# Root, tables, residual and last scaling around three RMS norms of a two-block float32 kernel: the epilogues reordered, and TensorE given products of ones

## What is computed

```python
def rmsnorm(x, g):
    return x * rsqrt(mean(x * x, axis=-1) + 1e-6) * g
# block 1, layer 0: convolution branch and gated linear recurrence, merged by w_out (tiles "ya", "yb")
x = x + gate0 * out_0
h1 = rmsnorm(x, norm_g[1]) * (1 + scale1) + shift1       # here called the first norm
# block 1, layer 1: pooling over a grid (tiles "ou", "og", "grp", "oa", "ob")
x = rmsnorm(x + gate1 * out_1, final_g)
# block 2: token mixers on h2 and a context (tiles "f" ... "gb2", "pa", "pb", "wo")
x = x + gate2 * mix
h3 = rmsnorm(x, g_ffn) * (1 + sc3) + sh3                 # here called the second norm
x = x + gate3 * ((silu(h3 @ w_a) * (h3 @ w_b)) @ w_down) # tiles "ua", "ub", then "d0", "d1", "d2"
out = rmsnorm(x, g_final)                                # the end
```

## Time and profile before

| what | value |
|---|---|
| median of 3 runs (lowest, highest) | 950.0 us (949.25, 951.11) |
| the profiled execution: its time, its span | 950.38 us, 948.6 us |
| PE busy; weight loads (PEld) | 891.7 us (94%); 833.6 us (88%) |
| DVE busy | 706.0 us (74%) |
| ACT busy; POOL busy | 500.6 us (53%); 142.0 us (15%) |
| mean granted clock of PE | 0.976 |
| the chain that ended last, by engine | PE 65%, DVE 20%, ACT 5%, issue 4%, DMA 3%, POOL 2% |

### The profile page before, as it was taken

One profiled execution on the slowest core, in us unless ns is written; L12 is line 12 of the kernel. 1 busy time (PEld: TensorE's weight loads), 2 busy tenths in 40 slices (PEclk: granted clock), 3 DMA queues, 4 the chain that ended last, 5 costly groups with the idle time before them and its releaser, 6 DMA issues.

```text
span 948.6 us, 17209 instructions
## 1 busy us (share of the span) xinstructions
PE 891.7 (94%) x7048; PEld 833.6 (88%) x7048; DVE 706.0 (74%) x1016; ACT 500.6 (53%) x717; POOL 142.0 (15%) x254
## 2 busy tenths in 40 slices
PE   6999999989997999899998999989999799999995
PEld 4788777778996998789998999979999699999995
DVE  4787678899876799988558985686985886666453
ACT  5475888796445544235543474563534454444441
POOL 0004675600011001400301100300001100000000
PEclk9999999999998999999999999989999799999998
DMA  9835987975575668775528844635556366666661
GB/s 370 354 133 161 291 271 230 296 281 177 160 264 200 222 224 278 255 266 178 178 73 286 290 131 137 201 94 194 157 179 178 121 235 179 186 188 181 198 200 47
DMA packets 56013, 195.53 MB, mean 206 GB/s; under 512 B 7936, under 2 KB 9088, under 8 KB 54528
## 3 DMA queue, kind: packets, MB, share of 16 engines
q1 hardware_dynamic: 40320, 147.83, 48.5%
q0 software_dynamic: 15616, 46.61, 14.5%
HBM read 188.70 MB, written 1.05 MB: 200 GB/s over the span
## 4 chain that ended last, share of the span: by engine, by line
PE 65%; DVE 20%; ACT 5%; issue 4%; DMA 3%; POOL 2%; DVEq 0%; ACTq 0%; SPq 0%; POOLq 0%
PE ps L570 18%; PE ps L571 18%; PE ps L572 18%; DVE w_lo L1333 6%; PE ps L721 3%; ACT w_hi L941 2%; DVE modw L1367 2%; POOL shifts L458 2%; DMA modw<-in_mod_w 2%; PE px L641 1%; DVE dump L1699 1%; DMA raw<-in_stream 1%; PE ps L652 1%; PE px L527 1%; DVE li L1347 1%
## 5 line engine op out<-in xcount | busy, mean ns | idle before, releaser
L1333 DVE TENSOR_TENSOR w_lo<-raw,w_hi 128x1024 fp32r<-128x1024 f32 x232 | 281.5, 1227 | 134.0 <-ACT w_hi L941 133.5
L941 ACT ACTIVATE w_hi<-raw 128x1024 fp32r<-128x1024 f32 x232 | 243.6, 1055 | 125.3 <-DMA raw<-in_stream 125.1
L570 PE MATMUL ps<-h_hi,w_hi 128*128 128x256 f32 (+1 forms) x928 | 278.8, 300 | 25.4 <-DVE w_lo L1333 12.1
L571 PE MATMUL ps<-h_lo,w_hi 128*128 128x256 f32 (+1 forms) x928 | 273.4, 295 | 0.0
L572 PE MATMUL ps<-h_hi,w_lo 128*128 128x256 f32 (+1 forms) x928 | 273.2, 294 | 0.0
L570 PEld LDWEIGHTS ps<-h_hi,w_hi 128*128 128x128 f32 x928 | 181.7, 196 | 37.8 <-DVE w_lo L1333 16.8
L571 PEld LDWEIGHTS ps<-h_lo,w_hi 128*128 128x128 f32 x928 | 181.9, 196 | 3.6 <-issue 1.2
L572 PEld LDWEIGHTS ps<-h_hi,w_lo 128*128 128x128 f32 x928 | 181.8, 196 | 2.6
L570 PE MATMUL ps<-h2o_hi,w_hi 128*128 128x256 f32 x352 | 103.5, 294 | 8.5 <-DVE w_lo L1333 8.5
L571 PE MATMUL ps<-h2o_lo,w_hi 128*128 128x256 f32 x352 | 101.4, 288 | 0.0
L572 PE MATMUL ps<-h2o_hi,w_lo 128*128 128x256 f32 x352 | 101.3, 288 | 0.0
(11 more groups left out here) (328 smaller groups left out, 1732.5 us busy)
## 6 DMA issues: line engine op xcount, KB each, us to landing
raw<-in_stream SPq DMA_DIRECT2D x252, 512.0 KB, 3.8
modw<-in_mod_w POOLq DMA_DIRECT2D x80, 512.0 KB, 6.2
m<-in_mod_w SPq DMA_DIRECT2D x8, 1024.0 KB, 18.1
shifts<-upad POOLq DMA_DIRECT2D x128, 35.5 KB, 4.3
c_row<-in_c_rows SPq DMA_DIRECT2D x3, 512.0 KB, 9.2
ctxT<-in_ctxT SPq DMA_DIRECT2D x1, 1024.0 KB, 4.9
x<-in_xT SPq DMA_DIRECT2D x1, 1024.0 KB, 7.0
ctx2T<-in_ctx2T SPq DMA_DIRECT2D x1, 1024.0 KB, 5.7
```

The costliest lines, as they stand in the source:

```text
L570: pe.matmul(o, wh, hi, start=start, stop=False)
L571: pe.matmul(o, wh, lo, start=False, stop=False)
L941: act.activation(w_hi[split[0] % HI_RING][:], raw[n % RING][:], ACT.Copy).then_inc(w_hi_ready, 1)
L1333: v.tensor_tensor(w_lo[n % RING][:], raw[n % RING][:], w_hi[split[0] % HI_RING][:].bitcast(F32), ALU.subtract).then_inc(w_lo_ready, 1)
```

## The change

1. **Root from the bank.** For the norms behind "yb", "og" (a norm of the second context), "wo" and "d2" DVE's mean plus epsilon is gone. ACT takes the root straight from PSUM, with 1/D as scale and a new column of 1e-6 as bias.
2. **Table ahead.** The dummy root that loads ACT's table is issued before the eight squares (for "og": directly before the root, without a wait between them) and no longer after them.
3. **Last residual ahead of the low half.** In `add_to_x` for the last slab of "yb" and "wo" DVE adds first, and makes the low half of the fourth tile of the next layer after it. For "ob" nothing changes, and for "d2" there is no low half left by then.
4. **Wide end.** ACT makes xg = x * g_final_2 in 8 instructions, one behind each square of "d2". DVE then multiplies xg by the reciprocal in three instructions, of 2, 3 and 3 slabs, and SP writes three times, 256, 384 and 384 KB.
5. **Ones.** At the first and the second norm PE multiplies the matrix of ones by itself (128 columns, into the bank px[1], which nobody reads) 4 times before `two_chunks` and 14 times after it.

The counts of the semaphore var_ready are lowered in the other norms to match.

```diff
+        xg = at("xg", W + 8, [KT, T])
...
-            for k in range(KT):
-                sp.wait_ge(stored, k + 1)
-                sp.dma_start(out[:, k, :], x[:, k, :]).then_inc(out_done, 16)
-            sp.wait_ge(out_done, 16 * KT)
+            for n, (first, end) in enumerate(((0, 2), (2, 5), (5, 8))):
+                sp.wait_ge(stored, n + 1)
+                sp.dma_start(out[:, first:end, :], xg[:, first:end, :]).then_inc(out_done, 16)
+            sp.wait_ge(out_done, 16 * 3)
...
+            def keep_busy(n):
+
+                for _ in range(n):
+                    pe.matmul(px[1][:, 0:P], ones, ones, start=True, stop=True)
...
+            keep_busy(4)
             two_chunks(px[0], sq1, 1, 3 * KT)
+            keep_busy(14)
             h1 = (lambda k: h1_hi[:, k, :], lambda k: h1_lo[:, k, :])
             side_by_side([("ou", t) for t in range(4)], *h1, (h_ready, 0))
...
+            keep_busy(4)
             two_chunks(px[0], sq4, 7, 7 * KT)
+            keep_busy(14)
...
+            def root_table():
+
+                S.do(act.activation(warm, warm, ACT.Sqrt))
+
+            def root_of_mean(stat, t, bank):
+
+                act.wait_ge(stat_done, stat)
+                act.activation(t, bank[:, 0:T], ACT.Sqrt, scale=1.0 / D, bias=eps_col).then_inc(sd_ready, 1)
...
+            root_table()
             for t in range(KT):
                 done("yb", t)
                 squares("yb", t, sq1)
-            highs("ou", 3)
-
-            sqrt_of(4, vr1[:])
+
+            root_of_mean(5, vr1[:], px[0])
             shifted(0, h1_hi, t1, shift1)
...
+            root_table()
             for t in range(KT):
                 done("wo", t)
                 squares("wo", t, sq4)
-            sqrt_of(10, v4[:, 0, :])
+            root_of_mean(9, v4[:, 0, :], px[0])
             shifted(3 * KT, h3_hi, t4, sh3)
...
+            root_table()
             for t in range(KT):
                 done("d2", t)
                 squares("d0", t, sq5)
-            sqrt_of(11, v4[:, 0, :])
+                act.activation(xg[:, t, :], x[:, t, :], ACT.Identity, scale=col("g_final_2", t)).then_inc(xg_ready, 1)
+            root_of_mean(10, v4[:, 0, :], px[0])
...
             def add_to_x(name, t, gate):
 
-                done(name, t)
+                if t < KT - 1 or name == "ob":
+                    ahead(name, t)
+                v.wait_ge(tile_done, TILE[(name, t)] + 1)
...
-            def rstd(stat, bank, width, eps, t, dst, var_n):
-
-                v.wait_ge(stat_done, stat)
-                v.tensor_scalar(t, bank, 1.0 / width, eps, ALU.mult, ALU.add).then_inc(var_ready, 1)
-                v.wait_ge(sd_ready, var_n)
+            def rstd(n, t, dst):
+
+                v.wait_ge(sd_ready, n)
                 S.do(v.reciprocal(dst, t))
                 S.sync()
...
-            rstd(10, px[0][:, 0:T], D, EPS, v4[:, 0, :], v4[:, 1, :], 11)
-            for k in range(KT):
-                v.scalar_tensor_tensor(out=x[:, k, :], in0=x[:, k, :], scalar=col("g_final_2", k), in1=v4[:, 1, :],
-                                       op0=ALU.mult, op1=ALU.mult).then_inc(stored, 1)
+            rstd(11, v4[:, 0, :], v4[:, 1, :])
+            v.wait_ge(xg_ready, KT)
+            for first, end in ((0, 2), (2, 5), (5, 8)):
+                by_token = v4[:, 1, :].rearrange("p (n t) -> p n t", n=1).to_broadcast([P, end - first, T])
+                v.tensor_tensor(xg[:, first:end, :], xg[:, first:end, :], by_token, ALU.mult).then_inc(stored, 1)
```

More of the change, by code:

```diff
@@ L361, in build @@
         out_done = sem("out_done")
+        xg_ready = sem("xg_ready")
         modA = columns(2 * KT).rearrange("p (k w) -> p k w", w=2)
@@ L372, in build @@
         ccs = columns(2 * KT)
-        warm = columns(1)
+        warm, eps_col = columns(1), columns(1)
         sc1, gate1 = columns(KT), columns(KT)
@@ L855, in _ @@
             thirds("ga2", 0, *own2)
-            pe.wait_ge(var_ready, 8)
+            pe.wait_ge(var_ready, 6)
             pe.wait_ge(hg_dve, 10)
@@ L885, in _ @@
             pe.wait_ge(in_sgu, 48)
-            pe.wait_ge(var_ready, 9)
+            pe.wait_ge(var_ready, 7)
             for g in range(HEADS):
@@ L1183, in _ @@
                 act.activation(og[:, t, :], psum_of("og", t)[:, 0:T], ACT.Silu).then_inc(free_of("og", t), 1)
-            sqrt_of(5, vr[:, 0, :])
+            root_table()
+            root_of_mean(6, vr[:, 0, :], px[1])
             for t in range(KT):
@@ L1195, in _ @@
             highs("f", 3)
-            sqrt_of(6, vr[:, 1, :])
-            act.wait_ge(var_ready, 7)
+            sqrt_of(4, vr[:, 1, :])
+            act.wait_ge(var_ready, 5)
             act.activation(vr[:, 2, :], vr[:, 2, :], ACT.Sqrt).then_inc(sd_ready, 1)
@@ L1275, in _ @@
             exps(1)
-            sqrt_of(8, lnv[:, 3, :])
+            sqrt_of(6, lnv[:, 3, :])
             out_of("o", 2, og2, ACT.Silu)
@@ L1300, in _ @@
             highs("gb2", 3)
-            sqrt_of(9, ors[:])
+            sqrt_of(7, ors[:])
             for t in range(KT):
@@ L1372, in _ @@
             v.memset(ones, 1.0).then_inc(cc_clear, 1)
+            v.memset(eps_col, EPS6)
             v.memset(warm, 1.0).then_inc(cc_clear, 1)
@@ L1669, in _ @@
             v.memset(opad[:, :, :, 8 + GRID_W:PW], 0.0).then_inc(pads_ready, 1)
-            rstd(5, px[0][:, 0:T], D, EPS6, vr1[:], vr1[:], 4)
+            rstd(4, vr1[:], vr1[:])
             modulate(0, x, vr1[:], sc1, shift1, t1, h1_hi, h1_lo)
@@ L1725, in _ @@
                     second_mods(g, s, 0, mod, t, True)
-            rstd(6, px[1][:, 0:T], D, EPS, vr[:, 0, :], vr[:, 3, :], 5)
+            rstd(5, vr[:, 0, :], vr[:, 3, :])
             for t in range(KT + 1):
@@ L1771, in _ @@
             v.tensor_scalar(vr[:, 0, :], vr[:, 1, :], EPS, None, ALU.mult).then_inc(var_ready, 1)
-            v.wait_ge(var_ready, 6)
+            v.wait_ge(var_ready, 4)
             v.wait_ge(stat_done, 8)
@@ L2033, in _ @@
             lows("ub", 1)
-            rstd(9, px[0][:, 0:T], D, EPS, v4[:, 0, :], v4[:, 1, :], 10)
+            rstd(10, v4[:, 0, :], v4[:, 1, :])
             modulate(3 * KT, x, v4[:, 1, :], sc3, sh3, t4, h3_hi, h3_lo)
```

## The result

The change takes 943.95 us (median of 4 runs, 942.41 to 944.51), the kernel before 949.62 beside it (4 runs). The ratio is 0.9933, 95% interval 0.9916 to 0.9951. The forecast was 944.4. The two medians lie 5.7 us apart. So the effect is rather 4 to 5 us than 5.7.

The account below looks back on a forecast made before the run. The prediction took PE, busy 94% of the span, as the bound. First norm 3.8, second norm 0.3 and end 1.5 sum to 5.6 us, from a median of 950.0 to 944.4; range 942.2 to 946.9.

Parts of the forecast that it names:

- First norm's chain: From "yb" to h at the first norm: the reciprocal starts earlier, 1.75 us gained.
- First norm's clock: Behind the first norm: PE's clock stays up, so the stretch at half clock takes half as long, 2.0 us gained.
- rival 4: Between "ou" and "grp" DVE's work swallows the first norm's 3.8 us: half, 946.3, or all, 948.2; chance 0.08.
- Rival 2: The ones don't hold PE's clock: at both norms 944.4, at the first only 946.5; chance 0.18.
- "og", 0, and tables ahead, 0: At "og" DVE gains about 0.9 us but PE doesn't wait; table loads ahead of the squares cost 0.
- Second norm's chain: From "wo" to h at the second norm: the reciprocal starts earlier, 2.4 us gained.
- "What is late next" at "ub" 2: Behind the second norm PE waits for DVE, about 4.2 us idle, then runs at half clock, 1.65 us lost.
- rival 1: No or only a short clock fall at "ub" 2: second norm gives 1.9 to 2.4 us, total 942.5; chance 0.14.
- gain of the second norm: Second norm with the wait at "ub" 2 behind it: 0.3 us gained net, between 2.4 and -1.5.
- The end: From the last sum to the last write: earlier root, wide products and larger packets, 1.5 us gained, between 0.6 and 1.85.
- Rival 3: At the end the writes are no faster by packet: 0.9 us less gain, 945.3; chance 0.1.
- Rival 5: At both norms each product of ones waits for the one before: 954.5; chance 0.04 together with no effect at all.

Follow-up runs that it names:

- change_again: The change itself, unaltered, run and traced a second time: 943.99 us against 949.10 for the kernel before, ratio 0.9959.
- eight_writes: Against the change: its three wide products kept, but the output written in eight transfers of 128 KB instead of three; 944.86 us, run once.

## Why the prediction was right, and where it was not

The total was right (944.4 against 943.95, 5.6 us against 5.7). The terms were not all right: in the first trace two errors of about 2 us offset each other, and that the total came out within half a microsecond is luck. In change_again's trace the second norm's term came out as forecast; the ratio of the repeat, 3.9 us, is lower than the forecast, but 5.6 lies in its interval.

**First norm's chain, 1.75.** Right: 1.83 by PE's way from the start of the last product of "yb" to h (8.23 and 6.40), and by the steps named; undoing the residual costs 0.9 and the tables 0.34 of it. The rest, some 0.6, I put down to the mean that is gone; no run undoes it alone.

**First norm's clock, 2.0.** Right: 1.86 in the stretch to "og", and it arrived, since from there to the end of "wo" the two traces, with the same course of the clock, differ by 0.12; rival 4 is out. Rival 2 is out at both norms.

**"og", 0, and tables ahead, 0.** Right: the stretch from "og" to the end of "wo" changed by 0.12. Back in their old place the tables cost 0.34, 0.56 and 1.0; the 1.5 that I gave as the price of being in the way was too high, since the sum covers a part.

**Second norm's chain, 2.4.** Right: 2.6. Undoing the residual costs 1.9 of it and the tables 0.6.

**"What is late next" at "ub" 2.** The place, the cause and the fall of the clock were right; rival 1 is out in all five traces that have the ones and the products in their place. The sizes were not. "I add 0.5, as the loads of the ring now start while half of the modulation weights are still under way" (bounds 0 and 1.3) measured 1.6 in the first trace (19.69 us from h to "ub" 2, not 18.09) and between 0.9 and 2.0 in the four others, over my upper bound in four of the five; in the first, VectorE waits 1.56 longer for its modulation loads. I had allowed for one ring load in front, but the four tiles behind the norm end together, so that more than one is asked for at once; that these are what delays the others I read from the 420 GB/s and didn't test alone. "1.65 lost" for the clock measured 2.6, or 1.4 in change_again: I took the half stretch behind "og", 3.3 us, for its length, and behind "ub" 2 it lasted 5.9 and 3.1. So the "gain of the second norm", 0.3, was a loss of 1.5 in the first trace and of 1.9 in eight_writes (6.19 + 199.57 against 8.80 + 195.09), and 0.3 gained in change_again. My lower end of -1.5 was itself summed wrong: 2.4 - 1.3 - 2.8 is -1.7. In the same way the upper end of the range, 946.9, should have been rival 2's 946.5.

**The end, 1.5.** The size is right: 1.55, of which the three transfers in place of eight are 1.0 (I had 0.9). Rival 3 is out as to the size. That it is the packets, as I wrote, is borne out for about half of it, by the estimate above; the pace of eight issues is a cause that I had not thought of.

**Sum.** The touched stretches give 1.86 + 1.86 - 1.54 + 1.55 = 3.7 in the first trace. The other 2.1 came in the main from the clock ahead of the first norm, for which I had no term: 1.5 behind the wait in "gb", and 0.5 up to there, where each of the two traces had lost time at another place. I made my sum against one trace of before and took its falls for the kernel's usual course. Rival 5 is out: 0.235 us for a product of ones.

## What to carry to other kernels

Filling a wait of TensorE with products that nobody reads kept its clock here at no cost, but it is worth something only if the next thing it needs is early enough; otherwise the wait and the fall move to the next place. Look there for work of the slower engine that nobody needs yet, and move that first: it was worth 6 to 8 us here, more than all five edits. Before summing terms against one trace, see which of its half-clock stretches another trace of the same program has too.

## What the runs showed of the hardware

- Whether the clock falls behind a short wait is not set by the wait's length. Behind the wait in "gb" (2.1 to 2.4 us) it fell in 7 of 13 traces, though the instructions around it are the same, and behind 4 us and more without ones it always fell. Near 20 us from the start it fell in 4 of the 13, in the change's first trace behind waits of 0.50 us only. It need not fall at once: behind the 1.88 us in "og" of before PE ran from 389.79 to 390.9 at full clock, and only then at half. How long it stays at half differs too, from 3.1 to 6.1 us behind "ub" 2. The Trainium skill (TensorE: Matmul & The Clock Gate, Part 1: The HAM clock gate) says that the number of products made at the lower clock at a kernel's start varies from run to run; the traces show the same in the middle of a kernel. A fall in "gb" costs 1.3 to 1.5 us, and the runs of one kernel spread by 3 to 10 us (940.6 to 951.0 for the change).
- Eight writes of 1 KB for each partition, issued 0.48 us apart, move at 261 GB/s with a DMA share of 0.78, and three of 2 and 3 KB at 366 with 0.92.
- A product of ones by 128 columns that writes the same bank as its predecessor costs 0.235 us (3.29 for 14), no more than the 0.24 (1.95 for eight) of products into two banks.
